# Sample key pieces moved ahead into the projection blocks and loaded by SyncE, cache copies regrouped, retention query products on four column tiles

## The reference, cut to what matters

```python
# sample attention, per group (window, dilation) = (128,1),(512,4),(2048,16)
kf = jnp.concatenate([buf[:, :, 0], k_new], axis=1)
kg = kf[:, idxc].astype(F32)                      # 129 keys for each of 4 tokens, 4 heads, 8 samples
s = jnp.einsum('bthd,btkhd->bthk', q.astype(F32), kg)
new_buf = jnp.concatenate([buf, jnp.stack([k_new, v_new], axis=2)], axis=1)[:, -Wb:]   # the cache shifted by 4
# retention, per sample (one chunk of 4 tokens)
o = jnp.einsum('bhij,bjhe->bihe', scores, vf)
o = o + jnp.einsum('bihd,bhde->bihe', qf, s0) * q_dec[None, :, :, None]
s1 = s0 * jnp.exp(log_gamma * C)[None, :, None, None] + jnp.einsum('bjhd,bjhe->bhde', kf * k_dec[None, :, :, None], vf)
```

## Time and profile before

| | us |
|---|---|
| median of 3 runs (lowest, highest) | 1094.57 (1094.48, 1100.29) |
| profiled execution: its time | 1096.48 |
| its span (first to last instruction) | 1094.7 |
| PE busy in the span | 1024.3 (94%) |
| DVE, ACT, POOL busy | 547.9, 380.4, 190.1 |
| mean granted TensorE clock | 0.979 of full |

### The profile page before, as it was taken

How to read it: one execution, slowest core, us unless ns; L and a number is a source line. 1 busy time by engine, 2 the same in 40 slices (tenths; PEclk the granted TensorE clock), 3 DMA queues, 4 the chain that set the end, 5 groups by cost and what they waited for, 6 DMA issues and landing times.

```text
span 1094.7 us, 20187 instructions
## 1 busy us (share of the span) xinstructions
PE 1024.3 (94%) x7698; PEld 889.5 (81%) x7698; DVE 547.9 (50%) x861; ACT 380.4 (35%) x834; POOL 190.1 (17%) x367
## 2 busy tenths in 40 slices
PE   5999999999997799999988888999999999999994
PEld 3777777778885699998877668999999999777773
DVE  5353223524236778665115366767676767422214
ACT  5333231341322333332213264444444443213312
POOL 2101002303132333333310100000000000111003
PEclk9999999999998899999899989999999999999998
DMA  6744425425486655664661522464545444221322
GB/s 223 264 156 165 156 105 194 176 83 204 153 297 209 195 184 190 200 199 133 221 215 58 197 78 73 172 218 154 181 157 205 166 170 137 87 83 63 105 94 85
DMA packets 40769, 175.35 MB, mean 160 GB/s; under 512 B 7243, under 2 KB 7691, under 8 KB 39169
## 3 DMA queue, kind: packets, MB, share of 16 engines
q1 hardware_dynamic: 25472, 125.79, 32.9%
q0 software_dynamic: 15232, 48.65, 13.9%
HBM read 164.41 MB, written 54.05 MB: 200 GB/s over the span
## 4 chain that ended last, share of the span: by engine, by line
PE 81%; DMA 6%; DVE 5%; ACT 3%; issue 2%; POOL 2%; SPq 0%; DVEq 0%; POOLq 0%; ACTq 0%
PE bank L1263 10%; PE bank L1265 10%; PE bank L1264 10%; PE bank L1741 8%; PE bank L1742 8%; PE bank L1743 8%; PE bank L1336 4%; PE bank L1338 4%; PE bank L1337 4%; PE bank L1282 3%; DMA qbc<-sample_queries 3%; DMA wraw<-in_weights 2%; PE bank L1429 2%; PE bank L1423 1%; DMA kvv<-in_cache_kv_g 1%
## 5 line engine op out<-in xcount | busy, mean ns | idle before, releaser
L1818 DVE TENSOR_TENSOR wlo<-wraw,whi 128x1024 fp32r<-128x1024 f32 x89 | 108.8, 1224 | 346.3 <-ACT whi L773 346.2
L773 ACT ACTIVATE whi<-wraw 128x1024 fp32r<-128x1024 f32 x91 | 96.4, 1059 | 393.2 <-PE bank L1265 255.6
L1741 PE MATMUL bank<-T1h,whi 128*128 128x288 f32 (+1 forms) x704 | 202.5, 288 | 3.1 <-DVE T1l L1828 1.7
L1742 PE MATMUL bank<-T1l,whi 128*128 128x288 f32 (+1 forms) x704 | 203.6, 289 | 0.0
L1743 PE MATMUL bank<-T1h,wlo 128*128 128x288 f32 (+1 forms) x704 | 203.1, 288 | 0.0
L1263 PE MATMUL bank<-whi,T1h 128*128 128x512 f32 (+1 forms) x352 | 142.2, 404 | 7.5 <-DVE etmp L1957 7.4
L1264 PE MATMUL bank<-wlo,T1h 128*128 128x512 f32 (+1 forms) x352 | 136.9, 389 | 0.0
L1265 PE MATMUL bank<-whi,T1l 128*128 128x512 f32 (+1 forms) x352 | 136.6, 388 | 0.0
L1741 PEld LDWEIGHTS bank<-T1h,whi 128*128 128x128 f32 x704 | 133.0, 189 | 3.8 <-issue 1.9
L1742 PEld LDWEIGHTS bank<-T1l,whi 128*128 128x128 f32 x704 | 132.7, 189 | 0.0
L1743 PEld LDWEIGHTS bank<-T1h,wlo 128*128 128x128 f32 x704 | 132.3, 188 | 0.0
(11 more groups left out here) (297 smaller groups left out, 1842.5 us busy)
## 6 DMA issues: line engine op xcount, KB each, us to landing
wraw<-in_weights SPq DMA_DIRECT2D x142, 512.0 KB, 3.6
out_s_kv_g<-in_cache_kv_g SPq DMA_DIRECT2D x64, 511.0 KB
qbc<-sample_queries POOLq DMA_DIRECT2D x48, 256.0 KB, 4.8
kvk<-in_cache_kv_g POOLq DMA_DIRECT2D x32, 256.0 KB, 4.4
kvv<-in_cache_kv_g POOLq DMA_DIRECT2D x16, 512.0 KB, 6.2
out_s_kv_g<-in_cache_kv_g SPq DMA_DIRECT2D x16, 508.0 KB
S<-in_state_ret POOLq DMA_DIRECT2D x16, 256.0 KB, 7.5
out_s_ret<-S POOLq DMA_DIRECT2D x16, 256.0 KB, 2.6
```

The source lines that it names most:

```text
L773: nc.scalar.activation(w_halves(s)[0], wraw[:, s % 2, :], ACT.Copy).then_inc(w_hi, 1)
L1741: mm(dst, Wh, T1h[:, k, c], start=k == 0, stop=False)
L1742: mm(dst, Wh, T1l[:, k, c], start=False, stop=False)
L1818: v.tensor_tensor(lo, wraw[:, s % 2, :], hi.bitcast(F), ALU.subtract).then_inc(w_lo, 1)
```

## The change

There are three edits.

1. **Key pieces.** The pieces are put in another order: pieces 0 to 31 are groups 0 and 1 of all eight samples, 32 to 47 are group 2. The first 32 run on DVE in the attention projection blocks, in eight lots of four (`PIECES_RET`, keyed by block and place in it): behind the third split and after `rope` in block 5, behind the first, second and third split and after `rope` in block 6, behind the first and second split in block 7. SP loads them, between its weight loads: slot 24, pieces 0 to 3, slot 25, pieces 4 to 7, and so on to slot 31 and pieces 28 to 31. They have buffers of their own. The last 16 pieces stay in the gate blocks (8) and in the first half of `S_GB` (8), and POOL loads them as before.
2. **Moves.** Two samples' caches are moved beside slots 2 to 21 in place of four beside 2 to 41; none beside slots 22 to 77; five beside slots 78 to 117 with eight slots each in place of ten; the last beside slots 120 to 141.
3. **Sample heads.** The eight `qm` products of a head go to four column tiles of bank 6 (rows 32p), in front of all `km` products in place of between them. ACT copies the first part (`os_first`), DVE adds the other three (L1984 of the changed kernel), and ACT's square for the norm moves to the next block.

```diff
+def key_piece(n):
+    if n < 32:
+        return n // 4, n // 2 % 2, 2 * (n % 2)
+    return (n - 32) // 2, 2, 2 * (n % 2)
...
-PIECES_RG = ((0, 3, 3), (3, 3, 2))
-PIECES_GB = (1, 3, 2, 2, 2, 3, 2, 2, 2, 3, 2, 2, 2, 2, 2, 2)
+PIECES_RET = {(5, 2): 4, (5, 4): 4, (6, 0): 4, (6, 1): 4, (6, 2): 4, (6, 4): 4, (7, 0): 4, (7, 1): 4}
+PIECES_RG = ((0, 2, 2), (2, 2, 0))
+PIECES_GB = (1, 1, 1, 1, 1, 1, 1, 1) + 8 * (0,)
...
+    def load_key_piece(eng, n):
+        b, g, t = key_piece(n)
+        keys, queries, _ = key_places(n)
+        keys_there, queries_there, _ = key_arrival(n)
+        if n >= 3:
+            eng.wait_ge(s_step, n - 2)
...
+        eng.dma_start(queries, src).then_inc(queries_there, 16)
...
+        load_beside_moves(2, 0, 2)
+        load(22)
+        sp.wait_ge(qs_out, 16)
+        for p in range(4):
+            for j in range(2):
+                load_one(24 + 2 * p, j)
+                for n in range(8 * p + 4 * j, 8 * p + 4 * j + 4):
+                    load_key_piece(sp, n)
+        with sp.Fori(0, (S_UP + 2 - 32) // 2) as it:
+            load(it * 2 + 32)
+        load_beside_moves(S_UP + 2, 2, 5)
+        load(118)
+        for e in range(11):
+            load(120 + 2 * e)
...
+            if bi == BLK_AV:
+                act.wait_ge(s_step, 32)
...
             pe.wait_ge(qm_ready, h + 1)
+            for e in range(2):
+                for p in range(4):
+                    if e == 0:
+                        pe.wait_ge(s0_in[p], 16 * (h + 1))
+                    last = mm(ob[32 * p:32 * p + TS, 0:DV], qm[:, h % 2, 2 * p + e, :], S0[:, p, e, :],
+                              start=e == 0 and p > 0, stop=e == 1)
+            last.then_inc(ofull, 1)
...
+            dve.wait_ge(os_first, h + 1)
+            b = filled(dve, ("Os", h))
+            out = vs[0:TS, DV * h:DV * h + DV]
+            for p in range(1, 4):
+                ins = v.tensor_tensor(out, b[32 * p:32 * p + TS, 0:DV], out, ALU.add)
```

More of the change, by code:

```diff
@@ L104, in value_piece @@
     return 2 * q + e, g
[L107 to L109 removed]
+def key_piece(n):
[5 more added lines that the diff above has]
+PIECES_GB = (1, 1, 1, 1, 1, 1, 1, 1) + 8 * (0,)
+assert sum(PIECES_RET.values()) == 32 and sum(map(sum, PIECES_RG)) + sum(PIECES_GB) == 16
 def psum_uses():
@@ L433, in build_layer @@
     q_in = [sem(f"q_in{n}") for n in range(3)]
+    kk_late, q_late = [sem(f"kk_late{n}") for n in range(3)], [sem(f"q_late{n}") for n in range(3)]
     s_step, pads_ready, qbd_ready, v_used, s_probs = (sem("s_step"), sem("pads_ready"), sem("qbd_ready"),
@@ L503, in _, with load_one @@
         sp.dma_start(convp[:], a["conv_params"]).then_inc(convp_in, 16)
+        def load_one(slot, j):
+            sp.wait_ge(w_lo, slot + (j - 1))
+            sp.wait_ge(w_seen, slot + (j - 1))
+            src = w_dram[bass.ds(slot + j, 1)].rearrange("a p n -> p (a n)")
+            sp.dma_start(wraw[:, j, :], src).then_inc(w_raw[j], 16)
         def load(slot):
             for j in range(2):
[L509 to L512, removed]
+                load_one(slot, j)
         def move(g, b, piece, pieces):
@@ L520, in move, with load_beside_moves @@
             sp.dma_start(cut(o[f"s_kv_g{g}"], 0), cut(kv_dram[g], DT * 512)).then_inc(windows_moved, 16)
[L523 to L528, removed]
+        def load_beside_moves(first, b0, batches):
+            with sp.Fori(0, batches) as it:
+                for e in range(5 if batches == 2 else 4):
+                    load(it * (10 if batches == 2 else 8) + (first + 2 * e))
+                    for piece in (((0, 1), (2, 3), (4, 5), (6,), (7,)) if batches == 2 else ((0, 1), (2, 3), (4, 5), (6, 7)))[e]:
                         move(2, it + b0, piece, 8)
[L530 to L533, removed]
+                    if e in (0, 3):
+                        move(1, it + b0, e // 3, 2)
+                    if e == 2:
                         move(0, it + b0, 0, 1)
[L536 to L541, removed]
+        load_beside_moves(2, 0, 2)
[12 more added lines that the diff above has]
+            load(120 + 2 * e)
+            if e < 8:
+                move(2, 7, e, 8)
+            elif e < 10:
+                move(1, 7, e - 8, 2)
+            else:
+                move(0, 7, 0, 1)
         sp.wait_ge(k_out, 16 * (NG + 2))
@@ L646, in _ @@
         pool.wait_ge(state_out_done, 16)
[L648 to L660, removed]
         pool.wait_ge(qs_out, 32)
         pool.wait_ge(k_out, 16 * (NG + 2))
-        for n in range(48):
-            load_piece(n)
+        for n in range(32, 48):
+            load_key_piece(pool, n)
         pool.wait_ge(s_step, 48)
@@ L1552, in sample_scores @@
             pe.wait_ge(s_step, 48)
-            turn(("st",), [sTk[:, g, :] for g in range(NG)], 128)
+            turn(("st",), [sT01[:, 0, :], sT01[:, 1, :], sT2[:, :]], 128)
             pe.wait_ge(qbd_ready, 1)
@@ L1929, in new_sample_states, with sample_piece @@
                 sample_queries(h + 2)
+            dve.wait_ge(os_first, h + 1)
[3 more added lines that the diff above has]
+                ins = v.tensor_tensor(out, b[32 * p:32 * p + TS, 0:DV], out, ALU.add)
+                if p < 3:
+                    step(ins)
+            ins.then_inc(bank_free[6], 1)
+        pieces = itertools.count()
+        def sample_piece():
+            n = next(pieces)
+            b, g, t = key_piece(n)
+            keys, queries, product = key_places(n)
+            keys_there, queries_there, count = key_arrival(n)
+            dve.wait_ge(keys_there, count)
+            dve.wait_ge(queries_there, count)
+            if n:
+                dve.wait_ge(s_step, n)
+            keys = keys[:, 0, :].unsqueeze(1).broadcast_to([128, 2, 256]) if g == 0 else keys
+            step(v.tensor_tensor(product[:].rearrange("p (t n) -> p t n", t=2), keys, queries, ALU.mult))
+            out = sT2 if g == 2 else sT01[:, g, :]
+            v.tensor_reduce(out[:, 16 * b + 4 * t:16 * b + 4 * t + 8], product[:].rearrange("p (k d) -> p k d", d=HD), AX.X,
+                            ALU.add).then_inc(s_step, 1)
         for bi in range(BLK_RG):
@@ L1939, in _ @@
                         state_update(bi - 4, s - 1)
+                for _ in range(PIECES_RET.get((bi, s), 0)):
+                    sample_piece()
             w_split(first + n + 1)
@@ L1944, in _ @@
                 rope(bi)
+            for _ in range(PIECES_RET.get((bi, n), 0)):
+                sample_piece()
             if bi == BLK_AV2:
@@ L1968, in gate_tile @@
             last.then_inc(r_ready, 1)
[L1970 to L1983, removed]
         for g in range(2):
@@ L2053, in _ @@
                 gated(n, gexp[:], 2, mixr[:, n, :], a_free[1])
-            for _ in range(PIECES_GB[s] - 1):
+            for _ in range(PIECES_GB[s]):
                 sample_piece()
```

37 lines of the change are left out of this document (26 added, 11 removed).

## The result

| | before | changed |
|---|---|---|
| median of 4 runs (lowest, highest), us | 1094.71 (1094.48, 1100.29) | 1120.12 (1119.05, 1122.64) |
| ratio, 95% interval | | 1.0224 (1.0204, 1.0245) |
| span of the profiled execution, us | 1094.7 | 1118.0 |
| mean granted TensorE clock | 0.979 | 0.966 |

The account below looks back on a forecast made before the run. PE was taken to set the time. Projection blocks cost 30.1 us more (36.3 idle + 5.4 clock - 11.6 heads), 22.1 won behind: +8.0 on 1096.48, 1104.5, less 1.9 for the median: 1102.5 us, range 1078 to 1118.

Parts of the forecast that it names:

- SP issues the load of slot 26 only after piece 7's DMAs: Block 6: these wait for DVE's piece 4, so the DMAs are issued by 12.6 us into the block, the load behind them.
- The idle time: Projection blocks 5 to 7: PE waits for late weight loads, 18.0 us in block 6, in all 36.3 us more.
- I take 4.4: Projection blocks: a weight load lands 4.4 us after issue, where the trace showed 3.5 to 7.1, median 4.5.
- The lower clock after the first idles and the heads lies under the next wait: Blocks 5 to 7: clock costs only behind the second idles of blocks 6 and 7, 2.7 us each, 5.4.
- The heads: Sample heads: query products on four column tiles save 2.9 us a head, 11.6 us in four.
- What is won behind: Gate blocks and sample scores: three old idles shrink and their clock loss goes, 22.1 us won.
- the 2.9: First gate idle, before the second gate block: 2.9 us of work lost to lower clock behind it, counted as won.
- The moves: Cache moves regrouped: 0 us, up to 3 beside the down projection if a load lands late.
- A: Projection blocks: weight loads land in time, DVE alone sets the pace; 1080 us, chance 0.20.
- B: Key pieces: keys land at 8.3 us, lengthening at least three lots; +15 us, 1118, chance 0.13.
- C: Sample heads: the four column tiles don't overlap; +6 us, 1108, chance 0.05.
- D: First gate block: late pieces still stall it, as POOL's first loads land late; +8 us, 1110, chance 0.07.

Follow-up runs that it names:

- e2: Changed kernel with SP's weight loads of slots 24 to 33 ahead of key DMAs that wait for a later piece: 1091.98 us, 0.9961 of the kernel before.
- e1: Kernel before with only the sample heads of the changed kernel: 1085.98 us, 0.9902 of the kernel before.
- e6: Changed kernel with the sample heads of the kernel before: 1123.18 us, 1.0242 of the kernel before.
- e8: As e4, but 20 key pieces in the projection blocks, 8 in the gate blocks, 20 beside the gate tiles: 1068.55 us, 0.9739 of the kernel before.
- e7: Kernel before with only the cache moves grouped as in the changed kernel: 1091.44 us, 0.9943 of the kernel before.
- e4: Changed kernel with SP's weight loads ahead of waiting key DMAs and four buffers for the first 32 pieces, not three: 1082.73 us, 0.9900 of the kernel before.
- e12: As e4, with the 32 pieces spread over seven places, none between rope and decayed: 1077.21 us, 0.9815 of the kernel before.
- e9: The kernel of e8 run again on another chip: 1070.60 us, 0.9763 of the kernel before.
- e11: The kernel of e4 run again: 1081.41 us, 0.9862 of the kernel before.

## Why the prediction was wrong in size

**The mechanism.** "SP issues the load of slot 26 only after piece 7's DMAs": right, at 12.6 us into the block as worked out, and right on who ends each idle, `PT` and `turn_evac`. What failed are sizes: the landing of a weight load, first of all, and three terms of the clock.

The Trainium skill (DMA: Bandwidth & Descriptors, Issuing engines are not separate DMA queues) holds that issuing DMAs on several engines at once saves only the time it takes to issue them. That rule prices the transfers, not what the issuing program waits for. In this case SP's issue of piece 7 takes 0.86 us and its waits cost 29 us (e2); no run changes the issuer alone.

**The idle time.** Forecast and measured: block 5's head 3.0 and 4.12; block 6 7.4, 6.9 and 4.2 against 7.94, 6.28 and 5.25; block 7 7.4, 6.9 and 1.5 against 10.26, 6.12 and 2.49. Less what stood there before, that is 36.3 forecast and 40.8 measured by the windows. The measured second idles look shorter than forecast only because the transposes in front of them ran at half clock, 2.79 in place of 1.47 us; with these 2.6 us the waits are 43.4, 7.1 more than forecast. The mis-sized term is "I take 4.4" for a weight load's landing. The tile `wraw` from 180 to 320 us, which answers to the earlier trace rows:

```profile
DMA to landing us min/median/max: 3.5/5.2/7.3
```

Seven loads lie on the chain of waits in blocks 5 to 7. They took 5.6 us in block 5, 4.9, 5.1, 5.3 and 5.2 in block 6, and 7.3 and 5.0 in block 7. The longest, that of slot 30, stood beside POOL's stores of the keys and SP's key DMAs. Above 4.4 each they take 7.6 us in all, which is the 7.1 and a little more.

**The clock.** "The lower clock after the first idles and the heads lies under the next wait", so 5.4 us in all, behind the second idles. The windows of the changed kernel from the first idle's end and from the second's, in block 6 and block 7:

```profile
227.60:236.70 9.10, 2.81 (x13) 2.44 (x13) 5.95 (x9) 1.76 (x5) 0.00 (x0) 0.50 0.71 209
236.70:245.60 8.90, 8.38 (x28) 6.54 (x28) 0.56 (x1) 1.84 (x8) 0.00 (x0) 0.62 0.16 53
...
295.10:304.00 8.90, 2.79 (x12) 2.41 (x12) 5.86 (x9) 1.65 (x3) 0.00 (x0) 0.69 0.66 210
304.00:313.40 9.40, 8.91 (x28) 6.90 (x28) 0.66 (x1) 1.70 (x4) 0.00 (x0) 0.59 0.16 53
```

and of the kernel before, the work that answers to the second and the fourth:

```profile
222.13:228.50 6.37, 5.47 (x28) 4.43 (x29) 0.57 (x1) 1.74 (x8) 0.00 (x0) 1.00 0.00 0
265.97:272.08 6.11, 5.47 (x28) 4.42 (x29) 0.62 (x1) 1.48 (x4) 0.00 (x0) 1.00 0.01 4
```

Behind the second idles PE is busy 8.38 and 8.91 us with what took it 5.47: 2.9 and 3.4 us are lost, not 2.7 each. The twelve transposes' loss is under the next wait, as said. But the `km` products behind a head's wait are the end of the block: in heads 1 and 2 they take 3.46 and 3.55 us (first of the idle rows above) in place of 2.0, and nothing hides these 3.0. For the heads that sentence is false. In all 9.3 us of clock lie in the open, 3.9 more than forecast. (With the transposes' 2.6 that is 11.9; the 11.5 of the windows takes 2.9 a head as saved, and the heads save a little more.)

**The heads.** 11.6 us less of PE's work: right, and e1 gives 10.2 by itself. In the changed kernel most of it comes back as waits (e6).

**What is won behind.** 22.1 forecast, 17.2 measured. The idles came as said: 7.42 to 1.07 (5.9 forecast, 6.35 won), 6.14 to 1.93 (4.7, 4.2), 2.51 to 0. The clock behind the first did not: 374.38 to 398.29 takes 23.9 us, and the same work took 22.4 before (340.17 to 362.58), so 1.5 us are lost where I had put 2.9 won. Two things are in this. The clock fell in this execution of the changed kernel, though the idle was gone (last section). And the 2.9 were never there to win. The same work before and in e8, where the clock stayed full:

```profile
340.17:362.58 22.41, 22.41 (x116) 16.76 (x116) 14.84 (x23) 4.30 (x6) 5.52 (x8) 0.87 0.70 220
...
323.28:345.12 21.84, 20.26 (x116) 15.31 (x116) 14.13 (x22) 5.15 (x6) 5.41 (x8) 1.00 0.58 176
```

Full clock wins 0.6 us, since PE then waits for DVE's `gate_tile`, which comes every 1.5 us either way; the timeline of PE in e8:

```profile
324.70 0.50 PE L1323 MATMUL bank<-whi,T1h 128*128 128x512 f32 x1 [0.48 <-DVE etmp L2048]
```

So 2.3 of the 4.4 us missing at this place are a price that took PE for the bound where DVE was, and 2.1 are the fall of the clock. From the second idle's start (362.58 and 398.29) to the value stage (545.68 and 570.99) 10.4 are won where I had 13.3, and 2.0 behind it that I had not counted.

**The moves.** "0" was wrong in itself: e7 gives 5 to 6 us. But what it shortens is the idle of 7.42 us, which the keys' move empties too (1.07 us are left in the changed kernel), so in the sum it should count once; the forecast erred in the reason and not in the time.

**The rivals.** A (loads in time, DVE alone sets the pace) did not come; it decides by when slot 26 is issued, and e4 is that case, 1081 to 1083, where A said 1080. B (keys land at 8.3) did not come: DVE waited 1.6 to 2.0 us for the fourth piece of most lots and 3.9 once, for piece 23, and there the weight load behind it was later still (DVE then waited 1.5 us for `whi`). C: the tiles overlap. D: the first gate block stalls by 1.07 us, as forecast.

In sum, of the 15.3 us between the forecast and the span, 7.1 are longer waits, for the landings of weight loads; 3.9 the clock in the blocks, 3.0 of it behind the heads, which was put at nothing; and 4.9 what is won behind, where the clock at one place took 4.4 and other terms 0.5. (That is 15.9; 0.5 come back in the heads and block 4.) The clock terms vary from run to run (below), so the split is that of one execution.

## What to carry to other kernels

A DMA that waits for its buffer blocks everything behind it in its engine's program. Before putting such loads between those that set the pace, write down for each what ends its wait, and sort the program by that, or give the loads as many buffers as a lot has pieces, so that none of a lot's DMAs waits for a piece of the same lot: here the one is worth 29 us, the other 25, and both 36 to 40. Where a stall is forecast, price the clock behind it too, and look whether the work at the lower clock ends the block or stands in front of another wait; and before counting a lower clock as a loss, look whether PE was the one that set the pace there.

## What the runs showed of the hardware

The same idle does not always cost clock. The idle of 1.07 us before the second gate block, with the same work on both sides and two shorter ones (0.3 to 0.6 us) in the 3 us behind it, was followed by a clock of 0.70 and 0.65 in the changed kernel's profile, and of 0.67 and 0.69 in that of e12, but by full clock in the eight others that have it (e2 to e6, e8, e9, e11; 0.94 us in e6). Two windows behind it in the changed kernel:

```profile
374.30:380.00 5.70, 4.59 (x12) 2.80 (x13) 5.59 (x12) 2.14 (x3) 0.00 (x0) 0.70 0.56 189
380.00:385.00 5.00, 5.00 (x17) 3.97 (x16) 0.82 (x1) 0.24 (x1) 0.00 (x0) 0.65 0.34 105
```

and in e8:

```profile
323.20:328.90 5.70, 4.04 (x14) 2.46 (x15) 5.59 (x12) 2.14 (x3) 0.00 (x0) 1.00 0.55 189
328.90:333.90 5.00, 5.00 (x24) 4.07 (x23) 2.05 (x3) 1.06 (x1) 0.00 (x0) 1.00 0.34 105
```

What decides it stays open: in all ten PE is busy without a break for the 12.9 us ahead of the idle, at full clock. And the executions of one kernel differ by it: e4's ten, on one chip, go from 1079.5 us at a mean clock of 0.987 to 1092.8 at 0.974. The 13.3 us between them are what 0.013 of the 1,015 us of busy PE would give, by my estimate. e8 and e9 are the same program on two chips, with spans of 1066.2 and 1070.9 at 0.990 and 0.984; of these 4.7 us 1.2 are idle in the first 20 us. So terms of clock of a few us, worked out from one execution as above, can be off by their own size.
